# State space tiles inside the projections of the late layers, loaded through the weight ring

## The reference, cut to what matters

```python
proj = rms_norm_2(h, g) @ w_in          # u_ssm 256 | u_g 256 | v_g 256 | q 512 | k 512 | v 512
# s5_mixer: 16 groups of 16 channels, 64 complex states each
bu = einsum(uf, b_bar)                   # channels to states
states = scan: state = a_bar * state + bu
y = real(einsum(states, c_mat)) + d_skip * uf
y = gelu(y); y = y * sigmoid(y @ w_glu + b_glu)
# spatial_gating: u_g * (W_s rms_norm(v_g) + b);  diff_attention: 4 heads x 2 halves, 128-query blocks
h = h + concat([y_ssm, y_sgu, y_diff]) @ w_out
```

## Time and profile before

| | us |
|---|---|
| median of 3 runs (lowest, highest) | 3074.41 (3071.2, 3075.0) |
| profiled execution: its time | 3073.82 |
| its span, first to last instruction | 3072.0 |
| PE busy in the span | 2920.0 |
| mean granted clock of PE, as a share of full | 0.974 |
| late layer 1: projections | 2408.0 to 2505.8 |
| late layer 1: from there to the first score | 2505.8 to 2534.5 |
| late layer 1: attention with the tiles | 2534.5 to 2642.7 |
| late layer 1: to the first matmul of w_out | 2642.7 to 2657.7 |

### The profile page before, as it was taken

The page is one execution under the profiler, slowest core; times in us unless marked ns, Lnnn a source line. Parts: engine busy times, 40 slices in busy tenths (PEclk is TensorE's granted clock), DMA queues, the critical chain, the costliest instruction groups (busy, mean ns, idle before and its releaser), DMA issues.

```text
span 3072.0 us, 38813 instructions
## 1 busy us (share of the span) xinstructions
PE 2920.0 (95%) x14757; PEld 2381.5 (78%) x14757; DVE 1083.7 (35%) x2145; ACT 709.7 (23%) x1735; POOL 1605.2 (52%) x1687
## 2 busy tenths in 40 slices
PE   6999999999999899999999898799999988899999
PEld 3545888888878799999999764588888764688887
DVE  1026643313255200000001238447264148357273
ACT  3135752101110111111110222432022222432020
POOL 0121027767778210107784543278788643378786
PEclk9999999999999899999999998899999989899999
DMA  6260013233442389999999303223333203133331
GB/s 184 61 186 25 15 29 97 89 108 95 124 122 91 96 240 265 263 261 267 299 301 309 111 31 114 63 83 93 106 93 106 79 31 136 45 94 96 102 93 52
DMA packets 543191, 388.07 MB, mean 126 GB/s; under 512 B 31178, under 2 KB 493221, under 8 KB 542488
## 3 DMA queue, kind: packets, MB, share of 16 engines
q1 hardware_dynamic: 523728, 327.85, 37.6%
q0 software_dynamic: 12832, 41.22, 4.0%
q10 hardware_dynamic: 6440, 16.44, 1.5%
HBM read 345.12 MB, written 40.80 MB: 126 GB/s over the span
## 4 chain that ended last, share of the span: by engine, by line
PE 88%; DVE 4%; ACT 3%; issue 2%; DMA 1%; SPq 1%; ACTq 1%; POOL 0%; another core or an unknown queue 0%; DVEq 0%; POOLq 0%
PE bank L593 17%; PE bank L594 17%; PE bank L595 17%; PE bank L728 15%; PE bank L1147 6%; PE bank L825 3%; PE bank L795 2%; PE bank L1221 1%; PE bank L813 1%; PE bank L1229 1%; PE bank L782 1%; PE bank L768 1%; DMA ring<-in_moe_w_down 1%; SPq L1286 1%; PE bank L891 1%
## 5 line engine op out<-in xcount | busy, mean ns | idle before, releaser
L1788 POOL TENSOR_TENSOR unit_parts<-ring,unit_parts 128x512 fp32r<-128x512 f32 x580 | 804.2, 1387 | 48.3
L1786 POOL TENSOR_SCALAR unit_parts<-ring 128x512 fp32r<-128x512 f32 x580 | 425.4, 734 | 538.4 <-PE bank L595 322.6
L593 PE MATMUL bank<-x_hi,unit_parts 128*128 128x512 f32 x1408 | 557.0, 396 | 16.5 <-DVE x L2234 10.3
L594 PE MATMUL bank<-x_lo,unit_parts 128*128 128x512 f32 x1408 | 550.6, 391 | 0.0
L595 PE MATMUL bank<-x_hi,unit_parts 128*128 128x512 f32 x1408 | 550.4, 391 | 0.0
L728 PE MATMUL bank<-arena,ring 128*128 128x160 f32 x2816 | 386.6, 300 | 3.5 <-ACT arena L1617 3.5
L728 PEld LDWEIGHTS bank<-arena,ring 128*128 128x128 f32 x2816 | 384.4, 191 | 3.9 <-ACT arena L1617 3.8
L593 PEld LDWEIGHTS bank<-x_hi,unit_parts 128*128 128x128 f32 x1408 | 265.7, 189 | 75.7 <-DVE x L2234 11.5
L593 PE MATMUL bank<-unit_parts,hid_parts 128*128 128x512 f32 x784 | 308.6, 394 | 9.2 <-DVE hid_parts L2256 9.2
L594 PEld LDWEIGHTS bank<-x_lo,unit_parts 128*128 128x128 f32 x1408 | 265.8, 189 | 57.0 <-issue 2.9
L595 PEld LDWEIGHTS bank<-x_hi,unit_parts 128*128 128x128 f32 x1408 | 265.8, 189 | 56.1
(11 more groups left out here) (311 smaller groups left out, 3665.2 us busy)
## 6 DMA issues: line engine op xcount, KB each, us to landing
ring<-in_moe_w_gate SPq DMA_DIRECT2D x88, 512.0 KB, 6.6
ring<-in_moe_w_up SPq DMA_DIRECT2D x88, 512.0 KB, 7.3
ring<-in_moe_w_down SPq DMA_DIRECT2D x64, 704.0 KB, 5.6
ring<-in_w_up SPq DMA_DIRECT2D x88, 512.0 KB, 5.1
ring<-in_w_down SPq DMA_DIRECT2D x16, 1024.0 KB, 5.1
ring<-in_od_w_in SPq DMA_DIRECT2D x24, 512.0 KB, 4.8
s_stream<-arena POOLq DMA_DIRECT2D x12, 1024.0 KB, 9.6
arena<-s_stream SPq DMA_DIRECT2D x16, 768.0 KB, 4.3
```

Of the source, the lines that this page charges most:

```text
L593: pe.matmul(ps, a[0], b[0], start=start, stop=False)
L594: pe.matmul(ps, a[0], b[1], start=False, stop=False)
L1786: pool.tensor_scalar(hi, raw, 1.0, 1.0, ALU.mult, ALU.mult).then_inc(S("units_rounded"), 1)
L1788: pool.tensor_tensor(lo, raw, hi.bitcast(F32), ALU.subtract).then_inc(S("units_split"), 1)
```

## The change

Each tile becomes a chunk of the weight ring: tables, the three matrices in, and three matrices out of 32 columns (`S5_ROW`, 2016 floats). `state_in` uses the 32 rows of `uT` that are the tile's channels, `state_out` writes 32 partitions of its bank, and `add_y` works on these 32 partitions. PE calls `next_state` (the way out of tile i-1, then the way in of tile i) after each chunk of `ugv` and `vd` and after the groups 1, 3, 5 and 7 of `normed`; the last way out comes after attention's first scores. The spatial gate stands before attention; its `vn` is scaled by DVE behind tile 4. One set of three buffers (`turned`) is used in place for the turned inputs, the scans and the products. POOL turns and sums the first four tiles between splits, the others behind its cosine products. The GLU comes after half-step 10 of attention. In the experts' stage, the output matrices are evicted in 16 small ACT operations for each of two rounds instead of four.

```diff
@@ -41,10 +41,11 @@
 HEAD_ROW = 6 * T + 32
 S5_TABS = 3 * T
 S5_MATS = 3 * P
-S5_ROW = S5_TABS + 2 * S5_MATS
+S5_GROUP = P // 4
+S5_ROW = S5_TABS + S5_MATS + 3 * S5_GROUP
 S5_ROUNDS = 2 * L2
-S5_BUFS = 3
-S5_STEPS = 3
+S5_EARLY = 4
+GLU_STEP = 10
 SLOTS = 5
 SLOT = KD * 256
 UNIT = SLOT // 4
...
 
-            def tmajor3(stage, s, kh, a_hi, a_lo, W, c0=0, halves=2, ready=None):
+            def tmajor3(stage, s, kh, a_hi, a_lo, W, c0=0, halves=2, ready=None, between=None):
...
+                        if between:
+                            between()
...
+                    if between and i < len(groups) and i % 2:
+                        between()
...
@@ -1179,9 +1177,44 @@
                 W = A["w_in_2"][l]
                 us = pair_chunk(f"in{l}", W[:, 0:P], W[:, P:2 * P])
                 first_pair(f"at{l}", [("u", l, 0), ("u", l, 1)], us)
-                tmajor3(f"in{l}", f"ugv{l}", KD, x_hi, x_lo, W, c0=256, halves=1)
-                tmajor3(f"in{l}", f"vd{l}", KD, x_hi, x_lo, W, c0=1792, halves=1)
-                s5_loads.append((len(chunks), l, 0, 1))
+                tile = [0]
+
+                def state_in(i):
+
+                    if i == 0:
+                        s5_first[len(chunks)] = l
+                        wait_drained(pe, ("u", l, 1))
+                    w = chunk((0, 1, S5_ROW, s5_dram[l, i]))
+                    s5_slot[l, i] = w, len(chunks) - 1
+                    q = slice(S5_GROUP * (i % 4), S5_GROUP * (i % 4 + 1))
+                    for m in range(3):
+                        ps = claim(("bu", l, i, m))
+                        fill(pe.matmul(ps[:, :], w[q, S5_TABS + m * P:S5_TABS + (m + 1) * P], uT[q, i // 4, :],
+                                       start=True, stop=True), ("bu", l, i, m))
+
+                def state_out(i):
+
+                    w, n = s5_slot[l, i]
+                    q = slice(S5_GROUP * (i % 4), S5_GROUP * (i % 4 + 1))
+                    ps = claim(("yp", l, i))
+                    pe.wait_ge(S("out_parts_ready"), 8 * l + i + 1)
+                    for m in range(3):
+                        at = S5_TABS + S5_MATS + S5_GROUP * (2 - m)
+                        ins = pe.matmul(ps[q, :], w[:, at:at + S5_GROUP], out_parts[m], start=m == 0, stop=m == 2)
+                    fill(ins, ("yp", l, i))
+                    chunks[n][2] = filled_sem(("yp", l, i))
+
+                def next_state():
+
+                    i = tile[0]
+                    tile[0] += 1
+                    if i:
+                        state_out(i - 1)
+                    if i < 8:
+                        state_in(i)
+
+                tmajor3(f"in{l}", f"ugv{l}", KD, x_hi, x_lo, W, c0=256, halves=1, between=next_state)
+                tmajor3(f"in{l}", f"vd{l}", KD, x_hi, x_lo, W, c0=1792, halves=1, between=next_state)
 
                 ps = claim(("wt", l))
                 pe.wait_ge(S("wn_ready"), l + 1)
...
-                normed(groups2(l), f"g2_{l}", mm2)
-
-                s5_loads.append((len(chunks), l, 1, 8))
+                normed(groups2(l), f"g2_{l}", mm2, next_state)
...
-                wait_drained(pe, ("u", l, 1))
-                state_in(0)
+                spatial_gate()
                 pe.wait_ge(S("rope_done"), 16 + 8 * (l + 1))
                 wait_drained(pe, ("dn", f"vd{l}", 0, NT - 1))
-                for i in range(8):
-                    if i < 7:
-                        state_in(i + 1)
-                    if i == 0:
-                        spatial_gate()
-                    if i:
-                        state_out(i - 1)
-                    attention(f"a2_{l}", S5_STEPS * i - 3, S5_STEPS * (i + 1) - 3)
-                state_out(7)
+                attention(f"a2_{l}", -3, 0)
+                next_state()
+                attention(f"a2_{l}", 0, GLU_STEP + 1)
                 w = chunk((0, 2, 256, A["ssm_w_glu_2"][l]))
-                attention(f"a2_{l}", 8 * S5_STEPS - 3, 8 * S5_STEPS - 2)
                 pe.wait_ge(S("yg_ready"), 2 * (l + 1))
                 for m in range(2):
                     ps = claim(("glu", l, m))
...
-                for at, l, i0, i1 in s5_loads:
-                    if at == n:
-                        load_s5(l, i0, i1)
+                if n in s5_first:
+                    sp.wait_ge(S(f"mats_stored{s5_first[n]}"), 16 * 2)
+                    sp.wait_ge(S(f"tabs_stored{s5_first[n]}"), 16 * 6)
...
+                    if q % 2 == 0:
+                        ins = act.activation(s5_turned[:, 4 * (i % 2):4 * (i % 2) + 4, (i // 2) * P:(i // 2 + 1) * P],
+                                             ps[:, :].rearrange("p (a b) -> p a b", a=4), ACT.Copy)
+                    else:
+                        for b in range(4):
+                            at = P * b + S5_GROUP * b
+                            ins = act.activation(
+                                s5_packed[:, 4 * (i % 2) + b, (i // 2) * S5_GROUP:(i // 2 + 1) * S5_GROUP],
+                                ps[:, at:at + S5_GROUP], ACT.Copy, scale=-1.0)
+                    drain(ins, key)
...
+                def turn_state(i):
+
+                    wait_drained(pool, ("bu", l, i, 0))
+                    pool.tensor_tensor(turned[1], turned[0], turned[1], ALU.add).then_inc(S("bu_turned"), 1)
+                    pool.tensor_tensor(turned[2], turned[0], turned[2], ALU.subtract).then_inc(S("bu_turned"), 1)
+
+                def sum_state(i):
+
+                    pool.wait_ge(S("scan_done"), 8 * l + i + 1)
+                    pool.tensor_tensor(z_sum, z_re, z_im, ALU.add).then_inc(S("z_sum_ready"), 1)
+
+                def late_state(i):
+
+                    (sum_state if i % 2 else turn_state)(S5_EARLY + i // 2)
+
+                split(f"in{l}", 12)
+                for i, stage in enumerate((f"in{l}", f"in{l}", f"qk{l}", f"qk{l}")):
+                    turn_state(i)
+                    split(stage, 2)
+                    sum_state(i)
+                    split(stage, 2)
+                rotary(groups2(l), f"g2_{l}", lambda l=l: split(f"qk{l}", 2), late_state)
 
...
+                    if 1 <= i <= len(groups):
+                        then(i)
...
+                drain(dve.scalar_tensor_tensor(out=yg[q, a, :], in0=uT[q, a, :], scalar=vcol("ssm_d_2", 2 * l + a)[q],
+                                               in1=ps[q, :], op0=ALU.mult, op1=ALU.add), key)
+
+            def turn_in(l, i):
+
+                tabs = s5_slot[l, i][0]
+                if i:
+                    add_y(l, i - 1)
+                for part, m, tab in ((0, 2, 0), (1, 1, 1), (2, 0, 2)):
+                    key = ("bu", l, i, m)
+                    ps = wait_filled(dve, key)
+                    drain(dve.tensor_tensor(turned[part], ps[:, :], tabs[:, tab * T:(tab + 1) * T], ALU.mult), key)
+
+            def scan_and_turn_out(l, i):
+
+                n = 8 * l + i
+                tabs = s5_slot[l, i][0]
+                rs = s5("r")[:, n:n + 1].broadcast_to([P, T])
+                dve.wait_ge(S("bu_turned"), 2 * n + 1)
+                dve.tensor_tensor_scan(z_re, rs, turned[1], 0.0, ALU.mult, ALU.add)
+                dve.wait_ge(S("bu_turned"), 2 * n + 2)
+                dve.tensor_tensor_scan(z_im, rs, turned[2], 0.0, ALU.mult, ALU.add).then_inc(S("scan_done"), 1)
+                dve.wait_ge(S("z_sum_ready"), n + 1)
+                dve.wait_ge(S("scan_done"), n + 1)
+                for m, z in enumerate((z_sum, z_re, z_im)):
+                    ins = dve.tensor_tensor(out_parts[m], z, tabs[:, m * T:(m + 1) * T], ALU.mult)
+                ins.then_inc(S("out_parts_ready"), 1)
 
...
+                for i in range(S5_EARLY):
+                    turn_in(l, i)
+                    scan_and_turn_out(l, i)
+
+                def late_state(i):
+
+                    k = S5_EARLY + (i - 1) // 2
+                    if i % 2:
+                        turn_in(l, k)
+                    else:
+                        scan_and_turn_out(l, k)
+                    if i == 2:
+                        dve.wait_ge(S("v_rms"), l + 1)
+                        for t in range(NT):
+                            dve.scalar_tensor_tensor(out=vn[:, t, :], in0=ugv[:, t, 256:512],
+                                                     scalar=s5("rstd")[:, t:t + 1], in1=vgain, op0=ALU.mult,
+                                                     op1=ALU.mult).then_inc(S("vn_ready"), 1)
+
+                normed2(l, rb, late_state)
                 dve.wait_ge(S("lam_exp"), l + 1)
                 tt(lam[:, 4:5], lam[:, 2:3], lam[:, 3:4], ALU.subtract)
                 tt(lam[:, 4:5], lam[:, 4:5], c("linit")[:, l:l + 1], ALU.add)
                 link(dve.tensor_scalar(lam[:, 5:6], lam[:, 4:5], -1.0, None, ALU.mult))
                 link(dve.tensor_copy(lam[:, 4:5], c("one")))
...
+                attention(f"a2_{l}", -3, 0)
                 for t in range(NT):
...
                 add_y(l, 7)
-                attention(f"a2_{l}", 8 * S5_STEPS - 3)
```

(34 more changed lines are left out.)

126 lines of the change are left out of this document (10 added, 116 removed).

## The result

| | us |
|---|---|
| kernel before, median of 4 runs (lowest, highest) | 3073.99 (3071.2, 3075.0) |
| changed kernel, median of 4 runs (lowest, highest) | 3131.04 (3127.72, 3133.13) |
| ratio, 95% interval | 1.0187 (1.0174 to 1.0200) |
| changed kernel, profiled execution: its time, span | 3127.72, 3125.9 |
| mean granted clock | 0.96 |

The kernel is slower by 57 us. The forecast was 3112 (+37), its range 3050 to 3138.

A forecast was written before the change was run, and what follows sets the result against it. It took DVE and its chain, not PE, to bound the woven attention and SSM stretch. Terms 38.7 - 15.4 - 49.2 + 39.6 + 5.0 = +18.7 us a layer, +37.4 for two, on 3074.4 gave 3112 us, range 3050 to 3138.

The forecast's parts named there:

- rival 1: DVE and POOL collide and PE waits in the late projections, as forecast: 3112 us, own range 3095 to 3135, chance 0.58.
- +38.7 for ways in and out: Late projections: eight ways in and seven out, 2.58 us each, add 38.7 us a layer where PE was full.
- -15.4 before attention: From the last SSM tile's way in to attention: 28.7 us becomes 13.3, 15.4 less a layer.
- -49.2 for attention alone: Attention without woven SSM tiles takes 59.0 us instead of 108.2, 49.2 less a layer.
- +39.6 for waits: Late projections: PE's waits for DVE's products of each tile add 39.6 us a layer.
- the ring as the second link: Tiles 4 and 5: w_in chunk loads wait for a ring slot, landing at +4.1; PE 8.5 us late, twice.
- "I take 2.0" for scans that collide: Late projections: a tile's two DVE scans lose 2.0 us against POOL's splits, from a possible 0 to 2.0.
- Rival 2: SSM scans don't collide with POOL in the late projections: 3084 us, chance 0.15.
- +5.0 for the clock: Late projections: half clock after PE's waits loses 1.0 us for each of five, 5.0 a layer.
- "Were PE never made to wait, a layer would be 25.9 us shorter": Late layers: without PE's new waits, each layer would be 25.9 us shorter than in the kernel before.
- rivals 3 and 4: Late projections: first, the chain fits, waits 17 us a layer, 3057, chance 0.14; second, waits all but vanish, 3023, chance 0.05.
- Covered edits: Experts' stage: twenty-four more small ACT evictions, taken as hidden; exposed, some 7 us at 0.3 each.

The follow-up runs named there:

- run 1: Changed kernel, but each tile's way-out matmuls read the sine table and identity, so PE doesn't wait for DVE's products; 3075.4 us, 1.0020 to the kernel before.
- runs 1 and 4: The second of the two: changed kernel, POOL sums before splits, and DVE scans tiles 4 to 7 right behind turn-in; 3074.9 us, 1.0008 to the kernel before.
- run 3: Changed kernel, with POOL summing each tile before it splits weight units; 3101.2 us, 1.0107 to the kernel before.
- run 6: Changed kernel, with POOL's splits in the late projections replaced by memsets that read nothing; 3082.0 us, 1.0055 to the kernel before.

## Why the prediction came out as it did

The direction and the mechanism were right, rival 1 is what happened; the size was 20 us short, and it came that near by errors that cancel. The projections stretch took 187.6 us where 181.1 were forecast: PE's work at full clock 142.3 and not 136.5, half clock 16.1 and not 5.0, waits 29.2 and not 39.6. The terms, for layer 1:

- **+38.7 for ways in and out**: mis-sized. In run 1 a chunk with a way out and a way in repeats every 2450.16 - 2433.57 = 16.59 us, so the pair costs 16.59 - 10.9 = 5.7, not 5.16: seven pairs make 3.7 more. In run 1 PE's whole work in the stretch was 145.8 us (147.2, less 1.4 for one way out at half clock) and not 136.5. Of these 9.3 us, another 1.7 are an `ms` and a rotation that stood behind the stretch's end before and stand inside it now, and some 3.2 are the half clock behind the ways in of tiles 0 and 3, which no term of mine had; 0.7 is left.
- **-15.4 before attention**: 14.6 us against 13.3. The gate ran at half clock (6.9). Small here, but it holds only while PE's waits stand ahead: without them DVE is late in the drain, 19.7 and 20.2 us in runs 1 and 4.
- **-49.2 for attention alone**: right, 59.3 against 59.0, the next stretch 15.0 as before.
- **+39.6 for waits**: too high by 11; 28.8 measured. Of that, 4.9 are the three stretches of half clock in the products, which moved from the waits into PE's own time. The early tiles were near (4.2 for 5.0). The first waited 0.75: POOL's second pair of splits had to wait for free units there and missed the products, 1.9, and 1.6 is half clock. Tiles 4 and 5 waited 6.6 and 5.3, not 8.5: w_in landed in 4.7 us (median), not 6.7, POOL's first split started at +3.2 and +3.4 from the mark instead of +4.1, and the scans began behind group 1's scaling in any case. I had named the ring as the second link; what ends last is DVE's order, as run 3 shows. That same order, which I had left out of tile 6, made 4.25 there instead of 2.2.
- **"I take 2.0" for scans that collide**: the end that I chose between 0 and 2.0 was the right one. The splits beside the scans lost 1.7 us in tile 1, and run 6 shows the mechanism. Rival 2 (3084) falls.
- **+5.0 for the clock**: too low. Six waits of 3.5 to 6.6 us lost 11.2 us on the ways out, 1.3 to 2.5 each, all above the 1.0 that I took and under the bound of 2.7. The stretches behind the ways in lost 4.9 more, but the waits behind them took that back.
- **"Were PE never made to wait, a layer would be 25.9 us shorter"**: this failed. Run 1's layers are 2.9 and 3.9 us shorter than before, in its fastest execution; by the medians the kernel is no shorter at all (1.0020). Of the 23 us between, 9.3 are PE's work, 5.6 idle time and 1.4 clock of waits that DVE's queue makes at `ms` and rotations, 6.4 the drain. So what a kernel without these waits would gain was put 23 us too high, and what the waits with their clock cost, net, was put at 44.6 where run 1 shows 30.2; the two errors hid most of each other, which was luck: 22.9 - 14.4 is the 8.5 us by which layer 1 came out above +18.7. It also means that rivals 3 and 4 had far less room than the text gave them: even with waits of 17 a layer (run 6 has 16.8) the kernel is 1.0055, not 3057.
- **Covered edits**: not settled. Sixteen of the small evictions take 1.55 us on ACT, far from the 0.3 each that I had as the price, but the medians leave 4 to 11 us outside the two layers that I can't place.

The profiled execution was 3.3 us under the median of its runs, so 54 of the 57 us are seen in it.

## What to carry to other kernels

Work moved under a full engine is paid twice: in that engine's own time, and in the dependent chain that now has to fit between two of its points. Write out that chain on every queue that it passes, and look what stands ahead of each of its links for no reason; here the order of a few instructions on POOL, DVE and PE turned 1.019 into 0.993 with the same work. Before counting on what a removed wait gives, ask who is late next: here the queue of DVE, at the rotations and in the drain.

## What was not expected of the hardware

- DVE's scan and POOL's elementwise operations take turns at SBUF reads: 1.19 to 1.22 us with POOL idle or only writing, 1.56 to 2.30 beside a POOL operation that reads, which itself goes from 0.62 to 1.53 or from 1.29 to 2.07.
- The half clock came without a wait too: in the projections of every profiled kernel with the change, one to three times a layer, matmuls fall to 0.43 us apart for about 3.4 us behind a tile's way in. In run 1 PE had waited for nothing in the 24.5 us before tile 0's way in. The projections of the kernel before show none. Whether the narrow matmuls, six fp32 passes in a row or something else brings it on was not tested, and stays open.
